# Three prompt tiles of a decoder step: gain applied per mix quarter, second norm folded into the turning products

## The reference, cut to what matters

```python
mix = merged @ p['w_out']
x = x + gt1 * _rmsnorm(mix, p['g_post_mix'])
h2 = _rmsnorm(x, p['g_pre_ffn']) * (1.0 + sc2) + sh2
f = _peer(h2, p['w_query'], p['sub_keys'], p['expert_u'], p['expert_v'])
x = x + gt2 * _rmsnorm(f, p['g_post_ffn'])
```

## Time and profile before

| | |
|---|---|
| median of three executions | 1892.54 us (1891.81 to 1894.42) |
| the profiled execution's own time | 1894.68 us |
| its span in the trace | 1892.9 us |
| TensorE / VectorE / ScalarE / GpSimd busy | 77% / 66% / 36% / 33% of the span |
| indirect gathers | 555.8 of 643.3 MB, 71% of the 16 DMA engines' time |
| mean granted TensorE clock | 0.82 |

### The profile page before, as it was taken

How to read it: one execution, slowest core, us unless ns; L and a number is a source line. 1 busy time by engine, 2 the same in 40 slices (tenths; PEclk the granted TensorE clock), 3 DMA queues, 4 the chain that set the end, 5 groups by cost and what they waited for, 6 DMA issues and landing times.

```text
span 1892.9 us, 23053 instructions
## 1 busy us (share of the span) xinstructions
PE 1459.0 (77%) x7760; PEld 687.4 (36%) x7760; DVE 1249.1 (66%) x2818; ACT 687.3 (36%) x1775; POOL 616.4 (33%) x590
## 2 busy tenths in 40 slices
PE   9999899999988898598777666656666575566665
PEld 4777678888734455243222110110110110000100
DVE  2077644776785657857767766677766777766765
ACT  3035444411444546624433332342332233222223
POOL 1100000000143334443434444444444445444442
PEclk9999999899999989688988677775676776666666
DMA  9533343213699999999999999999999999999997
GB/s 352 166 115 121 115 134 124 70 34 125 233 423 420 422 410 422 395 380 408 422 420 424 424 424 424 423 415 423 424 419 420 423 411 413 424 420 421 422 422 309
DMA packets 99910, 643.33 MB, mean 340 GB/s; under 512 B 11730, under 2 KB 11898, under 8 KB 31781
## 3 DMA queue, kind: packets, MB, share of 16 engines
q0 software_dynamic: 76912, 555.82, 71.1%
q1 hardware_dynamic: 22688, 85.96, 12.5%
q10 hardware_dynamic: 192, 0.09, 0.0%
HBM read 636.65 MB, written 6.18 MB: 340 GB/s over the span
## 4 chain that ended last, share of the span: by engine, by line
DMA 38%; PE 37%; DVE 9%; ACT 7%; issue 6%; POOL 2%; another core or an unknown queue 0%; DVEq 0%; ACTq 0%; SPq 0%; POOLq 0%
DMA arena<-in_euv,consts 38%; PE abank L867 22%; DVE arena L2209 4%; PE dbank L867 4%; PE dbank L1509 4%; PE fsum L1509 4%; ACT consts L835 2%; POOL arena L454 1%; PE abank L1404 1%; ACT small L831 1%; ACT arena L471 1%; ACT L736 1%; ACT arena L713 1%; PE fsum L907 1%; PE dbank L907 1%
## 5 line engine op out<-in xcount | busy, mean ns | idle before, releaser
L2209 DVE CUSTOM_DVE_ANT_0 arena<-arena 128x1024 f32<-128x1024 f32 x520 | 634.4, 1225 | 402.9 <-DMA arena<-in_euv,consts 395.9
L454 POOL DMA_INDIRECT arena<-in_euv,consts x520 | 584.3, 1124 | 765.2 <-PE fsum L1509 368.3
L867 PE MATMUL abank<-arena 128*128 128x256 f32 (+5 forms) x2448 | 541.1, 380 | 13.1 <-DVE arena L1768 3.8
L1509 PE MATMUL dbank<-arena,consts 128*32 128x512 f32 x1024 | 354.6, 849 | 216.5 <-ACT consts L835 213.7
L867 PEld LDWEIGHTS abank<-arena 128*128 128x128 f32 (+2 forms) x2448 | 404.2, 192 | 164.7 <-issue 69.2
L1509 PE MATMUL fsum<-arena,consts 128*32 128x512 f32 x1024 | 291.4, 789 | 169.3 <-ACT consts L835 166.2
L831 ACT ACTIVATE small<-small 128x1 f32<-128x1 f32 x520 | 104.7, 201 | 665.9 <-DVE small L2209 655.0
L1509 PEld LDWEIGHTS dbank<-arena,consts 128*32 128x32 f32 x1024 | 41.9, 125 | 497.0 <-ACT consts L835 483.8
L471 ACT ACTIVATE arena<-abank 128x512 f32<-128x512 f32 (+6 forms) x230 | 112.5, 489 | 282.4 <-PE abank L867 264.6
L835 ACT ACTIVATE consts<-arena,small 128x32 f32<-128x32 f32 x520 | 167.1, 321 | 17.5 <-ACT small L831 0.6
L1509 PEld LDWEIGHTS fsum<-arena,consts 128*32 128x32 f32 x1024 | 37.5, 121 | 369.7 <-ACT consts L835 349.6
(11 more groups left out here) (323 smaller groups left out, 1171.8 us busy)
## 6 DMA issues: line engine op xcount, KB each, us to landing
arena<-in_wstream SPq DMA_DIRECT2D x132, 512.0 KB, 4.8
arena<-in_euv,consts POOLq DMA_INDIRECT x520
arena<-in_wout SPq DMA_DIRECT2D x8, 1024.0 KB, 7.6
arena<-in_x SPq DMA_DIRECT2D x5, 512.0 KB, 6.3
arena<-in_sdel POOLq DMA_DIRECT2D x1, 2048.0 KB, 8.3
out_deltas<-arena POOLq DMA_DIRECT2D x1, 2048.0 KB, 11.9
out_yp<-arena SPq DMA_DIRECT2D x4, 512.0 KB
arena<-mod SPq DMA_DIRECT2D x3, 512.0 KB, 11.1
```

The source lines that it names most:

```text
L454: pool.indirect_dma_start(ring[n % SLOTS], None, I["euv"], bass.IndirectOffsetOnAxis(cur[:, u % 2, c:c + 1], 0)).then_inc(ring_in[n % SLOT ...
L867: return pe.matmul(out, lhsT, rhs, start=first, stop=last)
L1509: last = pe.matmul(out[e][to:to + 32, :], weighed, v, start=h == 0 and kk == 0, stop=h == PH - 1 and kk == 3, skip_group_check=True)
L2209: TTR(uh, uh, rep[j] if t < NT else h2sb, 1.0, 0.0, ALU.mult, ALU.add, dot[:, n // NQ % 2, n % NQ:n % NQ + 1]).then_inc(s.dots_done, 1)
```

## The change

For tiles 1 to 3 the second norm's scale and shift leave ACT, and for these and tile 4 the gain leaves the normal part:

- ACT takes the squares of each mix quarter at once (256 columns, `quarter_squares`) and adds the four sums in turn, where it took them over 1024 columns at the end.
- DVE multiplies each quarter with the gain in place (`later_gained`), two ticks behind the mix. The normal part is then one instruction that writes the sum to x, and a second one that writes x times the scale into `h2_all`.
- The turn multiplies this scaled x with the diagonal of inverse roots (now kept apart in `roots`) and adds the shift in PSUM by a second product of 16 rows. ACT empties two banks of 512 columns, plain.
- h2 in rows needs one DVE instruction instead of two.
- Tile 3's normal part, and the second part and the turn of tiles 1 to 3, stand one tick earlier, and `SPREAD` is drawn out: two at tick 24, one each at 27, 28, 30, 31, 56 and 58.

```diff
-        NORMAL = {37: 0, 38: 1, 40: 2, 42: 3}
-        SECOND = {39: 0, 41: 1, 43: 2, 44: 3}
-        TURN = {41: 0, 43: 1, 45: 2, 46: 3}
+        NORMAL = {37: 0, 38: 1, 40: 2, 41: 3}
+        SECOND = {39: 0, 40: 1, 42: 2, 43: 3}
+        TURN = {41: 0, 42: 1, 44: 2, 45: 3}
-        SPREAD = {24: (0, 1, 2), 25: (3, 4, 5, 8), 48: (6, 7)}
+        SPREAD = {24: (0, 1), 27: (2,), 28: (3,), 30: (4,), 31: (5,), 56: (6,), 58: (7,)}
...
+            def quarter_squares(n, e):
+                t, c = LATER[n], 4 * n + e
+                r, part = rows(t), parts_later[rows(t), c:c + 1]
+                before = parts_later[r, c - 1:c] if e else eps[r, :]
+                step(A(at(GB0 + 2 * D, 256)[r, :], h2_all[t][r, 256 * e:256 * e + 256], ACT.Square, accum_out=part), s.psq_ready)
+                if e < 3:
+                    step(A(part, part, ACT.Identity, bias=before, scale=1.0 / D))
+                else:
+                    step(A(rstd[r, t:t + 1], part, ACT.Sqrt, bias=before, scale=1.0 / D), s.mr_ready)
...
             def turned(t):
                 if t == NT:
                     empty(h2T[1][:, :, SEQ - P:], slice(0, KT * NB))
-                elif t == 0:
-                    for g in range(2):
-                        empty(h2T[0][:, 4 * g:4 * g + 4, :])
                 else:
                     for g in range(2):
-                        b = aring.to_read()
-                        for j in range(4):
-                            k = 4 * g + j
-                            s2, a2 = (mod_cols[:, k % 2, r + k // 2:r + k // 2 + 1] for r in (4, 8))
-                            step(A(h2T[1][:, k, (t - 1) * P:t * P], b[:, j * P:(j + 1) * P], ACT.Identity, bias=s2, scale=a2),
-                                 s.act_step if j < 3 else s.aring_free)
+                        empty(h2T[t > 0][:, 4 * g:4 * g + 4, max(t - 1, 0) * P:max(t, 1) * P])
...
                 for e, n in mixes_at(i):
                     mixed(LATER[n], e)
-                    if e == 3:
-                        means(LATER[n], h2_all[LATER[n]], at(GB0 + 2 * D, D))
+                    quarter_squares(n, e)
...
-                            last = mm(b[:, j * P:(j + 1) * P], x_t[:, t, k * P:(k + 1) * P], h2_all[t][:, 0:P])
+                            mm(b[:, j * P:(j + 1) * P], h2_all[t][:, k * P:(k + 1) * P], roots[LATER.index(t)], True, False)
+                            row = 4 + k // 2
+                            last = mm(b[:, j * P:(j + 1) * P], mod_rows[:, k % 2 * P:k % 2 * P + P],
+                                      consts[0:16, row:row + 1].to_broadcast([16, P]), False, True)
...
+            def later_gained(e, n):
+                dve.wait_ge(s.psq_ready, 8 + MIXES.index((e, n)))
+                step(TT(h2_all[t][r, here], h2_all[t][r, here], g1[r, here], ALU.mult))
...
-                step(STT(h, h, rstd[r, t:t + 1], g1, ALU.mult, ALU.mult))
-                step(TT(x_t[r, t, :], x_t[r, t, :], h, ALU.add), s.xs_ready)
+                step(STT(x_t[r, t, :], h, rstd[r, t:t + 1], x_t[r, t, :], ALU.mult, ALU.add), s.xs_ready)
+                step(TT(h, x_t[r, t, :], a2, ALU.mult))
...
-                    step(TS(h[:, 0:P], ident, rstd[:, t:t + 1], None, ALU.mult), s.h2_ready)
+                    step(TS(roots[LATER.index(t)], ident, rstd[:, t:t + 1], None, ALU.mult), s.h2_ready)
                     return
-                step(STT(h, x_t[r, t, :], rstd[r, t:t + 1], a2, ALU.mult, ALU.mult))
-                step(TT(h, h, s2, ALU.add), s.h2_ready)
+                step(STT(h, h, rstd[r, t:t + 1], s2, ALU.mult, ALU.add), s.h2_ready)
```

More of the change, by code:

```diff
@@ L233, in build @@
         parts4 = sm(206, 6)
-        mod_cols = sm(212, 32).rearrange("p (c r) -> p c r", r=16)
+        parts_later = sm(212, 16)
+        roots = [at(GA0 + D + P * n, P) for n in range(4)]
         dbank = [ctx.enter_context(nc.psum_tensor(f"dbank{i}", [P, 512], F32)) for i in range(4)]
@@ L359, in select_at @@
             return u + 1 < len(UNITS) and k == (3 if u == 0 else 2 if u + 1 == LATE else 0)
+        MIXES = [(e, n) for i in range(64) for e, n in mixes_at(i)]
         MEANS = []
@@ L772, in woven @@
                 for c in SPREAD.get(i, ()):
-                    if c == 8:
-                        empty(mod_cols, slice(0, 32))
-                        continue
                     v = (v_later + [v_g2])[c // 2]
@@ L1445, in woven @@
                         pe.wait_ge(s.mod_rows_in, 16)
[L1446 to L1452, removed]
+                    spread(c)
                 for e, n in mixes_at(i):
@@ L1971, in first_second @@
                     step(STT(h[:, half], h[:, half], rstd[:, 0:1], s2[:, half], ALU.mult, ALU.add), s.h2_ready)
+            def later_gained(e, n):
+                t, here = LATER[n], slice(256 * e, 256 * e + 256)
+                r = rows(t)
+                g1 = v_later[0] if t < NT else s_g1
+                dve.wait_ge(s.psq_ready, 8 + MIXES.index((e, n)))
+                step(TT(h2_all[t][r, here], h2_all[t][r, here], g1[r, here], ALU.mult))
             def normal_part(t, k):
                 r = rows(t)
-                h, g1 = h2_all[t][r, :], (v_later if t else v_first)[0] if t < NT else s_g1
+                h, a2 = h2_all[t][r, :], v_later[2] if t < NT else s_a2
                 inverse(t, k)
-                step(STT(h, h, rstd[r, t:t + 1], g1, ALU.mult, ALU.mult))
-                step(TT(x_t[r, t, :], x_t[r, t, :], h, ALU.add), s.xs_ready)
+                step(STT(x_t[r, t, :], h, rstd[r, t:t + 1], x_t[r, t, :], ALU.mult, ALU.add), s.xs_ready)
+                step(TT(h, x_t[r, t, :], a2, ALU.mult))
             def second_part(t, k):
@@ L1982, in second_part @@
                 h = h2_all[t][r, :]
-                s2, a2 = (v_later if t else v_first)[1:] if t < NT else (s_s2, s_a2)
+                s2 = v_later[1] if t < NT else s_s2
                 if k:
@@ L2179, in woven @@
                     other_gate(GATE_AT[i - 2])
+                for e, n in mixes_at(i - 2):
+                    if e + n == 0:
+                        dve.wait_ge(s.smod_in, 48)
+                        dve.wait_ge(s.later_ready, 2)
+                    later_gained(e, n)
                 if i in NORMAL:
@@ L2182, in woven @@
                         dve.wait_ge(s.xr_in, 32)
-                        dve.wait_ge(s.smod_in, 48)
                         dve.wait_ge(s.later_ready, 6)
```

## The result

The changed kernel takes **1913.9 us** (median of five executions, 1912.4 to 1915.0) against 1894.4 for the kernel before, executed beside it: ratio **1.0111** (95% interval 1.0098 to 1.0125), 19.5 us slower. The forecast was 1890.2, with a range up to 1895.3. The profiled execution took 1915.0 us, with a span of 1913.2.

What follows compares the result with a forecast made beforehand. The DMA stream of expert rows was taken as the bound, with a 7.9 us hole at 780 to 824 us. The walk's -2.3 and zeros for the rest took 1892.5 to 1890.2 us, range 1885.5 to 1895.3.

Steps and rivals of the forecast that it cites:

- What bounds the kernel: The DMA stream of expert rows at 424 GB/s; the hole at 780 to 824 us loses 7.9 us, the most winnable.
- the price of TensorE's turns: Turns of tiles 1 to 3, 32 records each: 6.3 us for the first two, 5.5 for the third.
- The walk: Ticks 42 to 48, through turns and query: tick 48's products at 811.7 instead of 814.0, a gain of 2.3 us.
- the middle one, 7.2: First query, ahead of tick 48's products: 7.2 us, taken from three instances of 8.51, 7.18 and 5.53.
- ACT's emptyings: Emptying of turned tiles: eight at 3.88 us become two at 1.29, 2.6 us less per turn, 7.8 for three.
- Spreads, quarter squares, DVE's gains: Work in the mixes and moved spreads, mostly ticks 24 to 31: each put at 0; DVE at worst 0.5 us.
- Rival D: Spreads in the mixes starve the stream, as TensorE has 5 us of pause in 80: 2 to 4 us, 1895.5; chance 0.05.
- Rival A: In the hole, turns fill idle places and TensorE's clock stays at 1.00: gain 6.3 us, 1886.2; chance 0.27.
- Rival B: Products of 16 rows don't count as work; turns 7.3 us, both queries 8.5: 4.1 us later, 1896.6; chance 0.12.

Runs made afterwards that it cites:

- all-16-row kernel: Changed kernel with both products of each pair over 16 rows, most of the sum left out, so output wrong: 1898.8 us, ratio 1.0044.
- whole-row kernel: Changed kernel with the shift's product over 128 rows instead of 16, adding a wrong shift: 1891.6 us, ratio 1.000.
- kernel without shift products: Changed kernel with the 16-row shift products left out, so queries of tiles 1 to 3 lack the second shift: 1889.9 us, ratio 0.9984.
- grouped order: Changed kernel with each bank's four products of x first and its four 16-row shift products behind them: 1897.6 us, ratio 1.0030.
- 64 rows: Changed kernel with each pair's second product over 64 rows instead of 16, shift wrong: 1910.4 us, ratio 1.0113.
- the last version: Changed kernel with rows of tiles 1 to 3 made whole on VectorE and turned plainly: 1887.4 us, ratio 0.9995; again 1889.4, 0.9998.
- The shift on ScalarE: Changed kernel with the shift given back to ACT as bias of eight emptyings a turn, the diagonal kept: 1891.2 us, ratio 1.0009.
- warm start: Changed kernel plus ten 128-row products in TensorE's idle time at the start of tick 42, before the first turn: 1907.4 us, ratio 1.0098.

## Why the prediction was wrong

**What bounds the kernel** was read rightly, as far as a loss goes. The stream lost 17.0 us more in 780 to 830, and the medians differ by 19.5. That a microsecond won there is a microsecond of time is not shown by any complete version.

**The step that failed is the price of TensorE's turns**: "A turn of 32 thus costs 5.3, 7.3 or 4.6 us". It carried records of whole 128-row products over to a stream in which every second product has 16 rows. Measured 11.6, 11.6 and 11.6 against 6.3, 6.3 and 5.5: 16.6 us too little. Two things stand behind it:

- the changes of row count: 16 a turn x 0.295 = 4.7 us at 1.2 GHz. 32 x 0.2135 + 4.7 = 11.5.
- the clock: 32 x 0.2135 = 6.8 us (7.1 with the turn's ends in the all-16-row kernel) where whole rows come up to speed inside the turn and take 5.0, 4.3, 3.8.

Over three turns that is 14.2 us for the first and 7.4 for the second, 21.6 above the whole-row kernel's 13.1. The forecast's 18.1 already stood 5.0 above these 13.1, since it took part of the turns at the lower clock, and so 16.6 were missing. The sentence "the nearest, with 256, is 2.21/8 = 0.276 us a record, no cheaper than a whole one" compared a record of 256 columns with whole ones of 128, and bounded the wrong thing besides. The spreads it comes from are eight 16-row records in a row. A bound for a 16-row record was there; none for the change between two kinds was. The range was built on durations of whole records, and so had no end on this side.

**The walk** held up where no turn was in it and the clock did not matter: tick 44's products came 4.5 us behind turn 1's end, where the forecast had 4.6 (788.2 - 783.6). It gave the first query at 804.5; with the 16.6 of the turns that is 821.1, and 822.4 was measured. So close a fit is luck, since two errors nearly cancel. The first turn began at 775.2, 2.1 us ahead of the forecast's 777.3 (in the traces of the other kernels with a diagonal in the turn it began between 774.7 and 780.3). And the diagonal products ran at a granted clock of 0.50: 2.3 us instead of 1.2 for tick 44's, 1.9 instead of 1.1 for tick 45's, 3.8 from the last turn to the query instead of 2.2, together 3.5 us more. "With no more long pause before it I take the middle one, 7.2" was too much: the first query took 5.6 us in the changed kernel, and 5.5 in most of the others. That is 1.6 us less than the forecast had.

**ACT's emptyings** are 1.2 us, as priced (1.29), and won nothing: ACT stands 5.3 us before each second one. In the kernel without shift products ACT's saving shows: the query starts at 800.7.

**Spreads, quarter squares, DVE's gains** were put at 0, and the 660 to 740 row agrees: 415 GB/s as before, with ACT busy 43.6 us there instead of 33.2, DVE 53.1 instead of 47.7. Rival D is out.

**Rival A** (1886.2) is what the rest of the change does with whole or no shift products, as far as the trace of that stretch goes: turns of 3.8 to 5.3 (2.0 to 3.6 without shift products), a query of 5.5, 390 to 403 GB/s. The time did not follow (1889.9 to 1891.6, with the kernel before at 1889.6 to 1892.0). In the changed kernel itself TensorE was at work for every microsecond of the turns and the clock did not come up. By the rule of activity that the prediction took from the Trainium skill ("TensorE: Matmul & The Clock Gate", "What's actually happening") it should have. Whole rows followed it, 16 rows did not.

**Rival B** named the mechanism that decided the clock, "products of 16 rows don't count as work", and priced it at 4.1 us with turns of 7.3. That fits the clock alone, which with no change inside the turn gave 7.1; it lacked the price of a change, and both together gave 11.6. Its argument against itself, "half of the records are whole ones", is true of the grouped order: there the clock rose in the second turn. In the alternating order with 16 rows it never did.

The Trainium skill, "TensorE: Matmul & The Clock Gate", section "LDWEIGHTS (loading the stationary operand)", says that a load takes its time by columns and that the number of rows doesn't matter. The trace agrees for the load itself: 0.50 us for a pair of loads over 16 or over 128 rows. What mattered is where the load stands. With equal rows it begins 0.2 us before its own product (in the whole-row kernel a load at 776.26 for the product at 776.47), with unequal rows together with it. The same page of the Trainium skill, section "The mechanism", says that a load is pulled ahead of running products if its row groups don't conflict or it goes to the background buffer. The trace agrees that loads are pulled ahead, by 0.2 us where the rows are equal; which groups or buffers they use no run here shows.

**What stays open.** Whether it is the count of rows that holds the load back, or the size of the block of weights, rows or columns. The turn's ends speak for the size. The third turn of the kernel without shift products has 128 rows before it, in it and behind it, and only the weights' columns go from 32 to 128 and back:

```profile
793.40 2.05 PE L868 MATMUL abank<-arena 128*128 128x128 f32 x16
795.38 1.07 PE L1504 MATMUL fsum<-arena,consts 128*32 128x512 f32 x8
```

It takes 1.98 us, which is 16 x 0.111 and 0.20, the price of one change at this clock, and in the whole-row kernel the load at the start of its third turn begins with its product, at 792.51. No run tests columns by themselves, and of rows only 16 and 64 beside 128 were run.

How much of the low clock comes from the few rows and how much from the slower pace is open too. The all-16-row kernel has few rows at full pace and stayed at 0.50. At the same 0.208 us a record, the clock was kept with 64 rows in the one execution traced and fell with 16, so the pace is not all of it.

And it is open whether the 5.7 us that the last version wins in 780 to 830 are given back at all. The 356 GB/s they are counted from are those of one execution, which took 1894.7 us, 5 more than the 1889.6 that the kernel before took beside the last versions. Trace against trace, the two executions of the rows whole on VectorE are 2.9 and 7.2 us shorter. The shift on ScalarE has a place where it loses: 395 GB/s over 660 to 740 instead of 415, which is 80 x 20/424 = 3.8 us.

## What to carry to other kernels

A product added for "a little sum" is priced by its neighbours, not by its size: look whether the products before and behind it have the same number of rows. If they don't, pad it to the same rows (with zeros and a unit column the ratio to the kernel before was 1.0006 instead of 1.0111), or put products of one kind together (1.0030). When you bound an operation that the trace lacks by the nearest row, ask what stood before and behind that row too.

## What the runs showed of the hardware

- A change of row count between successive products (128 and 16) costs 0.29 us at a granted clock of 0.50 (changed kernel, grouped order) and 0.19 to 0.20 at 1.00 (64 rows, warm start, grouped order). The float32 record of 128 columns is 0.2135 and 0.111 us without it (whole rows).
- With equal rows a weight load begins 0.2 us ahead of its own product (whole rows, 776.26 and 776.47), at a change of rows together with it (changed kernel, 775.92), although the load itself takes 0.50 us a pair at 16 and at 128 rows.
- Records over 16 rows alone, TensorE busy 10.00 of 10 us, leave the granted clock at 0.50 over three turns; in alternation with whole ones it falls from 1.00 to 0.50 without a pause; whole rows in the same place raise it within the first turn.
- With 64-row products in alternation the time was 1893.7 in one execution, with the clock up from the first pair on, and 1910 to 1913 in four. That the clock made the difference is argued: the four have no trace.
